# VectorE's order inside gate pairs changed, and sparse attention's angles made one down part earlier

## The reference, cut to what matters

```
def swiglu(h, w1, w3, w2):
    return (jax.nn.silu(h @ w1) * (h @ w3)) @ w2

def rope_tables(positions, rot_dim):
    inv_freq = ROPE_THETA ** (-jnp.arange(0, rot_dim, 2, dtype=jnp.float32) / rot_dim)
    ang = positions.astype(jnp.float32)[..., None] * inv_freq
    return jnp.cos(ang), jnp.sin(ang)
...
    h = modulate(x, norm_g[l, 0], mod[:, 0, 0], mod[:, 0, 1])
    x = x + 0.5 * mod[:, 0, 2][:, None, :] * swiglu(h, ffn1_w1[l], ffn1_w3[l], ffn1_w2[l])
    h = modulate(x, norm_g[l, 1], mod[:, 1, 0], mod[:, 1, 1])
    y = hybrid_mixer(h, ..., rope_a, rope_i, top_k)
    x = x + mod[:, 1, 2][:, None, :] * y
    h = modulate(x, norm_g[l, 2], mod[:, 2, 0], mod[:, 2, 1])
    x = x + 0.5 * mod[:, 2, 2][:, None, :] * swiglu(h, ffn2_w1[l], ffn2_w3[l], ffn2_w2[l])
```

## Time and profile before

| | us |
|---|---|
| median of 3 runs | 1863.03 (1861.79 to 1863.89) |
| the profiled execution | 1862.07 |
| its span | 1860.30 |
| PE busy | 1837.5 (99%) |
| DVE busy | 1334.8 (72%) |
| ACT busy | 857.3 (46%) |
| POOL busy | 270.8 (15%) |

### The profile page before, as it was taken

How to read it: one execution, slowest core, us unless ns; L and a number is a source line. 1 busy time by engine, 2 the same in 40 slices (tenths; PEclk the granted TensorE clock), 3 DMA queues, 4 the chain that set the end, 5 groups by cost and what they waited for, 6 DMA issues and landing times.

```text
span 1860.3 us, 27681 instructions
## 1 busy us (share of the span) xinstructions
PE 1837.5 (99%) x10112; PEld 1530.2 (82%) x10112; DVE 1334.8 (72%) x2105; ACT 857.3 (46%) x1545; POOL 270.8 (15%) x248
## 2 busy tenths in 40 slices
PE   9999999999999999999999989999999999999999
PEld 7777778888888888798988968757767889899897
DVE  7778456757766666896985886866785788689394
ACT  6465445433232233452643554446655455355262
POOL 0001000001111000151532310100000103154140
PEclk9999999999999999999999999999999999999999
DMA  5211113346666563423332122211111422322213
GB/s 187 91 57 68 60 67 115 136 135 235 227 224 224 183 213 106 159 79 110 114 107 84 49 91 91 82 64 50 47 57 69 159 95 78 135 91 103 85 52 102
DMA packets 58325, 208.25 MB, mean 112 GB/s; under 512 B 6688, under 2 KB 6816, under 8 KB 58208
## 3 DMA queue, kind: packets, MB, share of 16 engines
q1 hardware_dynamic: 47232, 167.67, 26.0%
q0 software_dynamic: 10976, 39.00, 6.4%
HBM read 204.48 MB, written 2.10 MB: 111 GB/s over the span
## 4 chain that ended last, share of the span: by engine, by line
PE 79%; DVE 14%; issue 5%; ACT 1%; DMA 0%; SPq 0%; DVEq 0%; ACTq 0%
PE PS L726 16%; PE PS L728 15%; PE PS L727 15%; DVE LO L2962 5%; PE PS L1451 4%; PE PS L1452 4%; PE PS L1453 4%; PE PS L1223 2%; PE PS L1438 2%; PE PS L1440 2%; PE PS L1439 2%; PE PS L1263 2%; PE PS L1250 1%; DVE LO L2153 1%; DVE HL L3009 1%
## 5 line engine op out<-in xcount | busy, mean ns | idle before, releaser
L1542 ACT ACTIVATE HI<-RAW 128x1024 fp32r<-128x1024 f32 x237 | 250.5, 1058 | 326.9 <-PE PS L728 206.6
L2153 DVE TENSOR_TENSOR LO<-RAW,HI 128x1024 fp32r<-128x1024 f32 x237 | 290.7, 1227 | 131.1 <-ACT HI L1542 129.7
L726 PE MATMUL PS<-XH,HI 128*128 128x512 f32 x848 | 337.9, 398 | 0.0
L728 PE MATMUL PS<-XH,LO 128*128 128x512 f32 x848 | 330.8, 390 | 0.0
L727 PE MATMUL PS<-XL,HI 128*128 128x512 f32 x848 | 330.4, 390 | 0.0
L726 PEld LDWEIGHTS PS<-XH,HI 128*128 128x128 f32 x848 | 159.2, 188 | 39.2 <-issue 7.8
L728 PEld LDWEIGHTS PS<-XH,LO 128*128 128x128 f32 x848 | 159.2, 188 | 34.4
L727 PEld LDWEIGHTS PS<-XL,HI 128*128 128x128 f32 x848 | 159.4, 188 | 31.0
L1438 PE MATMUL PS<-TH,HI 128*128 128x256 f32 x576 | 163.8, 284 | 5.0 <-DVE Y L3037 5.0
L1439 PE MATMUL PS<-TL,HI 128*128 128x256 f32 x576 | 163.0, 283 | 0.0
L1440 PE MATMUL PS<-TH,LO 128*128 128x256 f32 x576 | 162.9, 283 | 0.0
(11 more groups left out here) (478 smaller groups left out, 3853.3 us busy)
## 6 DMA issues: line engine op xcount, KB each, us to landing
RAW<-weights SPq DMA_DIRECT2D x237, 512.0 KB, 3.5
ADA<-ada POOLq DMA_DIRECT2D x72, 512.0 KB, 4.5
SRAW<-weights SPq DMA_DIRECT2D x72, 512.0 KB, 4.3
y_out<-X SPq DMA_DIRECT2D x8, 256.0 KB, 2.0
X<-x_in SPq DMA_DIRECT2D x3, 512.0 KB, 7.6
RAW<-weights SPq DMA_DIRECT2D x4, 256.0 KB, 5.5
X<-x_in SPq DMA_DIRECT2D x2, 256.0 KB, 4.5
COND<-condition POOLq DMA_DIRECT2D x1, 512.0 KB, 4.6
```

What stands on the lines that cost most here:

```text
L726: mm(bank, a, moving[0][:, t, :], start=start, stop=False)
L728: ins = mm(bank, z, moving[0][:, t, :], start=False, stop=stop)
L1542: A(HI[n0 % 3][:], RAW[n0 % 3][:], ACT.Copy).then_inc(sem("hi_ready"), 1)
L2153: V.tensor_tensor(LO[n0 % 3][:], RAW[n0 % 3][:], HI[n0 % 3][:].bitcast(F32), ALU.subtract)\
```

## The change

Four things move, and no matmul, transfer or POOL instruction does.

1. Angles. They are made in the second down part of f = 1 (down products 1 and 4) and kept in `T[:, 1, :]` and `UP_ZERO`. The conversion of the positions stands in its down product 0. The tables stay in the third down part, from products 0 and 2 to 1 and 3, behind the copies for the norm.
2. Finishing products. The three multiplies L3024, L3032, L3041 become two: the whole `H[0]` (128x512) behind c12, and the late half of `H[1]` behind A22's own multiply (`last_quarter`, two products behind).
3. Low parts. They go from three products behind to six: the low part of `H[0]` (`low_of_first`) now comes in the next gate pair, the low part of `H[1]` (`low_of_second`) in front of the next odd c11. At the end of a part all that is left comes behind the last A22.
4. ACT. The early silu of a gate pair and the high part of `H[1]` come four products behind in place of two.

The waits that keep buffers apart change with it: A11 of an odd pair waits for `h21_made`, c11 and c22 of odd pairs for low parts of the tiles before, c22 of even pairs for the last multiply.

```diff
+        ANGLE = [Y[:, 0, :], Y[:, 0, :], T[:, 1, :], UP_ZERO[:]]
...
                     elif kind == "A11" and p > 1:
-                        pe.wait_ge(sem("hid"), hid_count(f, pair_tile(p - 2, 1)))
+                        pe.wait_ge(sem("h21_made"), NPAIRS // 2 * (f - 1) + p // 2)
...
                         if s > 2 * v0 + 1:
                             later(f, s - 2)
+                        if s > 2 * v0 + 3:
+                            silu_of_first(f, s - 4)
+                            high_of_second(f, s - 4)
...
-                            if m in (0, 2):
+                            if m in (1, 3):
+                                act.wait_ge(sem("hid_lo"), FT * f + FT)
                                 table(2 + m // 2, (TAB_A2, TAB_I2)[m // 2])
...
                 if kind == "A12":
                     v.wait_ge(*product_done(f, kind, p))
                     v.wait_ge(sem("p1_copied"), of_pair(f, p))
+                    if p % 2:
+                        v.wait_ge(sem("hid_lo"), split_count(f, pair_tile(p - 2, 0)))
                     V.tensor_tensor(dst[0][:, EARLY], P1C, bank, ALU.add).then_inc(sem("c11_made"), 1)
-                    if p % 2:
-                        v.wait_ge(sem("c11_made"), of_pair(f, p))
-                        v.wait_ge(sem("part_silu"), part_silu(f, p, 1))
-                        V.tensor_tensor(H[0][:, EARLY], H[0][:, EARLY], G[0][:, EARLY], ALU.mult)
...
-                        V.tensor_tensor(H[0][:, LATE], H[0][:, LATE], G[0][:, LATE], ALU.mult)\
-                            .then_inc(sem("hid"), 1)
+                        V.tensor_tensor(H[0], H[0], G[0], ALU.mult).then_inc(sem("hid"), 1)
...
+                    if p % 2 == 0 and p:
+                        v.wait_ge(sem("hid"), hid_count(f, pair_tile(p - 1, 1)))
+                    elif p:
+                        v.wait_ge(sem("hid_lo"), split_count(f, pair_tile(p - 2, 1)))
                     V.tensor_tensor(dst[1][:, LATE], P5C, bank, ALU.add).then_inc(sem("c22_made"), 1)
-                    if p % 2:
-                        v.wait_ge(sem("c22_made"), of_pair(f, p))
-                        v.wait_ge(sem("part_silu"), part_silu(f, p, 3))
-                        V.tensor_tensor(H[1][:, LATE], H[1][:, LATE], G[1][:, LATE], ALU.mult)
...
+            def last_quarter(f, s):
+
+                kind, p = PRODUCTS[s]
+                if kind == "A22" and p % 2:
+                    v.wait_ge(sem("c22_made"), of_pair(f, p))
+                    V.tensor_tensor(H[1][:, LATE], H[1][:, LATE], G[1][:, LATE], ALU.mult).then_inc(sem("hid"), 1)
...
-                        if s > 2 * v0 + 2:
-                            later(f, s - 3)
+                        if s > 2 * v0 + 1:
+                            last_quarter(f, s - 2)
+                        if s > 2 * v0 + 5:
+                            low_of_first(f, s - 6)
+                            low_of_second(f, s - 6)
...
                     after_product(f, 2 * v1 - 1)
-                    for s in range(2 * v1 - 3, 2 * v1):
-                        later(f, s)
+                    last_quarter(f, 2 * v1 - 1)
+                    for s in range(2 * v1 - 6, 2 * v1):
+                        low_of_first(f, s)
+                        low_of_second(f, s)
...
-                        if squares and m == 0:
+                        if part == 1 and f == 1 and m == 0:
                             v.wait_ge(sem("pos_loaded"), 32)
                             link(V.tensor_copy(POS2[:], POS2[:].bitcast(I32)))
-                            angles(2, POS2[:], "freq_a")
-                        if squares and m == 2:
-                            angles(3, POS2[:], "freq_i")
+                        if part == 1 and f == 1 and m in (1, 4):
+                            angles(2 + m // 4, POS2[:], ("freq_a", "freq_i")[m // 4])
```

More of the change, by code:

```diff
@@ L1683, in later @@
                 kind, p = PRODUCTS[s]
-                if p % 2 == 0 and kind == "A12":
-                    act.wait_ge(sem("c11_made"), of_pair(f, p))
-                    A(G[0][:, EARLY], G[0][:, EARLY], ACT.Silu).then_inc(sem("part_silu"), 1)
-                elif p % 2 == 0 and kind == "S4":
+                if p % 2 == 0 and kind == "S4":
                     act.wait_ge(sem("c12_made"), of_pair(f, p))
@@ L1692, in later, with silu_of_first, high_of_second @@
                     A(G[1][:, LATE], G[1][:, LATE], ACT.Silu).then_inc(sem("part_silu"), 1)
-                elif p % 2 and kind in ("S4", "A22"):
-                    m = int(kind == "A22")
-                    hidden_hi(f, pair_tile(p, m), H[m])
+                elif p % 2 and kind == "S4":
+                    hidden_hi(f, pair_tile(p, 0), H[0])
+            def silu_of_first(f, s):
+                kind, p = PRODUCTS[s]
+                if p % 2 == 0 and kind == "A12":
+                    act.wait_ge(sem("c11_made"), of_pair(f, p))
+                    A(G[0][:, EARLY], G[0][:, EARLY], ACT.Silu).then_inc(sem("part_silu"), 1)
+            def high_of_second(f, s):
+                kind, p = PRODUCTS[s]
+                if p % 2 and kind == "A22":
+                    hidden_hi(f, pair_tile(p, 1), H[1])
             def whole_silu(f, t, bank, dst):
@@ L1730, in ffn_by_pairs @@
                     later(f, 2 * v1 - 2)
-                    later(f, 2 * v1 - 1)
+                    for s in range(2 * v1 - 4, 2 * v1):
+                        silu_of_first(f, s)
+                        high_of_second(f, s)
                     for m in range(DT):
@@ L1759, in table @@
             def table(k, tab):
+                angle = ANGLE[k]
                 act.wait_ge(sem("angle"), k + 1)
-                A(tab[:, 1, :], Y[:, 0, :], ACT.Sin)
-                A(Y[:, 1, :], Y[:, 0, :], ACT.Abs).then_inc(sem("absolute"), 1)
+                A(tab[:, 1, :], angle, ACT.Sin)
+                A(Y[:, 1, :], angle, ACT.Abs).then_inc(sem("absolute"), 1)
                 act.wait_ge(sem("absolute"), k + 1)
@@ L2312, in angles @@
             def angles(k, pos, freq):
-                if k % 2:
+                if k == 1:
                     v.wait_ge(sem("table"), k)
@@ L2321, in angles @@
                                                 op0=ALU.mult, op1=ALU.add))
-                V.tensor_scalar(Y[:, 0, :], Y[:, 1, :], 3.1415925, -3.1415925, ALU.min, ALU.max)\
+                V.tensor_scalar(ANGLE[k], Y[:, 1, :], 3.1415925, -3.1415925, ALU.min, ALU.max)\
                     .then_inc(sem("angle"), 1)
@@ L3044, in after_product, with low_of_first, low_of_second @@
                     v.wait_ge(sem("part_silu"), part_silu(f, p, 4))
-                    V.tensor_tensor(H[1][:, EARLY], G[1][:, EARLY], bank, ALU.mult).then_inc(sem("hid"), 1)
-            def later(f, s):
+                    V.tensor_tensor(H[1][:, EARLY], G[1][:, EARLY], bank, ALU.mult).then_inc(sem("h21_made"), 1)
+            def last_quarter(f, s):
                 kind, p = PRODUCTS[s]
-                if p % 2 and kind in ("S4", "A22"):
-                    m = int(kind == "A22")
-                    hidden_lo(f, pair_tile(p, m), H[m])
+                if kind == "A22" and p % 2:
+                    v.wait_ge(sem("c22_made"), of_pair(f, p))
+                    V.tensor_tensor(H[1][:, LATE], H[1][:, LATE], G[1][:, LATE], ALU.mult).then_inc(sem("hid"), 1)
+            def low_of_first(f, s):
+                kind, p = PRODUCTS[s]
+                if p % 2 and kind == "S4":
+                    hidden_lo(f, pair_tile(p, 0), H[0])
+            def low_of_second(f, s):
+                kind, p = PRODUCTS[s]
+                if p % 2 and kind == "A22":
+                    hidden_lo(f, pair_tile(p, 1), H[1])
             def whole_hidden(f, t, bank, gate):
@@ L3066, in hidden_zero @@
                     v.wait_ge(sem("unrooted_copied"), 4 * f - 2)
-                    V.tensor_tensor(UP_ZERO[:], UP_ZERO[:], PS[:, 6, :], ALU.mult).then_inc(sem("up_scaled"), 1)
+                    link(V.tensor_tensor(UP_ZERO[:], UP_ZERO[:], PS[:, 6, :], ALU.mult))
                 elif m == 3:
                     v.wait_ge(sem("silu"), FT + 4 * f)
-                    v.wait_ge(sem("up_scaled"), f)
                     V.scalar_tensor_tensor(out=T[:, 0, :], in0=UP_ZERO[:], scalar=SHIFT_COL[1], in1=T[:, 0, :],
```

## The result

| | before | after |
|---|---|---|
| median of 5 runs (us) | 1863.24 (1861.79 to 1863.95) | 1854.81 (1851.76 to 1856.11) |
| span of the profiled execution | 1860.3 | 1853.9 |

The ratio is 0.9949, with an interval of 0.9936 to 0.9963, and the medians lie 8.4 us apart. The forecast was 1855.4, with a range of 1851.0 to 1861.5.

What follows compares the result with a forecast made beforehand. PE bounds the kernel, busy 1837.5 of 1860.3 us. Angles 5.6, S1's copy 3.6, A22 1.8, down starts -3.4 give 7.6 us gained: 1854.5, and 1855.4 with the median 0.96 above the profiled execution; range 1851 to 1861.5.

Steps and rivals of the forecast that it cites:

- Angles: Third down part, first layer: two waits (2.8 and 1.2 us) and a half-clock stretch (1.6) go, 5.6 us gained.
- ScalarE's order: Gate pairs: moving silu and high part behind S2's copy ends 8 waits of S4 for S1's copy, 3.6 us gained.
- The pairs together: Up and gate pairs: two terms, 3.6 us from S1's copy waits and 1.8 from A22's waits for c22.
- The walk of VectorE: VectorE's instructions between c22s in the new order: 11.01 us even to odd, 9.53 odd to even, double pair 20.54.
- What L3024 gives: Up pairs: removing this VectorE multiply gives about 0.6 us of its 1.34, bounds nothing to 1.38.
- Rival 1: Pairs: L3024 gives its whole 1.38 us and A22 waits nowhere; 13.2 us gained, 1849.8 us; chance 14%.
- Rival 2: Pairs give nothing, L3024 wholly under POOL, or lower clock follows idle time at down starts; 1862.0 us; chance 15%.
- Rival 3: VectorE's double pair grows to 21.62 us through the new low part and POOL; slower, 1866.6 us; chance 9%.
- The down starts: Start of the first two down parts, both layers: longer chain behind A22 costs 1.45 us in place of 0.6, 3.4 lost.
- The norm: Norm behind the third down part: its half-clock stretch may fall elsewhere, 1 us left either way.

Runs made afterwards that it cites:

- E1: Kernel before with only the angles moved to the second down part, as in the change; 1857.24 us, ratio 0.9965.
- E9: Kernel before with only ScalarE's early silu of the gate pairs put four products behind in place of two; 1862.43 us, ratio 1.0001.
- E5: Kernel after with the early silu of the gate pairs back two products behind, high part of the second tile left four behind; 1854.0 us, ratio 0.9955.
- E10: Kernel after with the three multiplies and ScalarE's order of before, keeping the new places of angles and low parts; 1858.46 us, ratio 0.9968.
- E7: Kernel before with POOL's four sums of each pair replaced by writes of zeros, so only its times are read; 1850.49 us, ratio 0.993.
- E6: Kernel after with the wide multiply of the first tile split into two narrow ones, behind c11 and c12; 1856.18 us, ratio 0.9964.
- E3: Kernel after with the last pair's first-tile low part right behind its c22 at the end of the first two parts; 1846.94 us, ratio 0.9918.

## Why the prediction was right, and where it was not

The total was right, 1855.4 against 1854.81. By stretches the gain is 9.6 us against the 7.6 of the sum, so that the median came within 0.6 us is partly luck: the terms were off by up to 1.5 us, and the start and the norm, which no term describes, scatter by more than 0.6. Most of the mechanism was as forecast, one attribution was wrong, and several sizes were off.

**Angles, -5.6.** Measured -5.86 (E1 alone -5.86), with nothing lost in the second down part. All three pieces went: the 2.8 of waiting, the stretch at 0.50, and the 1.03.

**ScalarE's order, -3.6.** This step failed, and the total doesn't show it, since VectorE's new order took the same waits away. The waits went, as forecast, but not by this cause: E9 made the same move alone and got 1.0001, with the waits moved to A22 of the gate pair. E5 undid it and lost nothing, and in E10 the waits went without it. The forecast's own paragraph on VectorE said that VectorE sets the pace and that PE's waits are its backlog. It should have asked of every wait in the pairs, not only of A22's, whether it is backlog. What the 8 waits are worth here is what VectorE's double pair gets shorter by (21.30 to 20.6), and the silu's place didn't change that.

**The pairs together, -3.6 and -1.8.** Measured -6.9, 1.5 more than the two terms. The walk of VectorE was right where the backlog stands: 11.01 and 9.53 forecast, 11.02 and 9.59 measured between pairs 9 and 11. What was mis-sized is which pairs reach it. Against E7, where no product waits, a layer of before loses 5.5 us (forecast 5.6) and one of after 2.0 (forecast 2.9): 1.4 of it in pairs 0 to 3, as forecast (1.4), but 0.6 in pairs 4 to 11 (forecast 1.1) and none in 12 to 17 (forecast 0.4). I let VectorE start the second up pair of a part with the full 11.01, but c22 of pair 7 came 10.42 behind that of pair 6.

**What L3024 gives, 0.6.** E6 measures 0.34, its 1.34 us in the profile notwithstanding. It lies within the bounds of 0 and 1.38, nearer to the lower. The rule of the Trainium skill (SBUF — State Buffer, Who interferes with whom), that a VectorE instruction with two SBUF inputs and a GpSimd one that reads SBUF exclude each other, was the better guide here, and E7 agrees with it: with POOL only writing, 0.42 in every pair. Rival 1, which took the 1.34 for work, is refuted by the same runs. Rival 2, by which nothing of L3024 comes back, was about as far off on this size as the forecast (0.34 measured, against 0 and 0.6), but the other moves of the pairs, by subtraction above all the last multiply's, gave what rival 2 denied them, and PE's new idle time at the down starts, 1.45 us, was not followed by a lower clock. Rival 3 needed a longer double pair than 21.30; it was 20.6.

**The down starts, +3.4.** Measured +4.06, 1.02 in each place against 0.85. From A22's first matmul to the down product it is 3.11 us, 1.67 more than its 12 x 0.12, where I had 1.45. The chain of L3059, L3066 and one low part is as forecast; the 0.19 from the end of A22's last 0.12 us (962.48) to L3059 (962.67) was left out. E3 shows that the term was no part of the price of the change: the instruction's earlier place was free.

**The norm.** 0.8 us of the gain lies there, inside the 1 us that the forecast left for it: the half clock stretch is not in the kernel after, yet it is in E1, whose third down part is as short, and in eight more of the 13 traces behind the same 1.7 us of idle time. No edit accounts for it.

## What to carry to other kernels

Where one engine's queue sets the pace, a wait of the engine that it feeds marks a place and not a cause: take away what it names, and the same time comes back at a later product (E9). So price a change by how much it shortens the pacing engine's time over one turn of the loop, here a double pair. The profile's length of an instruction is no measure of what its removal gives when another engine holds it; look for the next instruction that will be held. And when instructions are queued later to relieve a loop, look at the loop's end by itself: there the same instruction is on the path, and an exception to the new order for the last pass gave 6.4 us more (E3).

## What the runs showed of the hardware

- A VectorE multiply with both inputs in SBUF, 128x256, took 0.42 us alone and 1.34 (L3024) to 1.52 (L3066 at 945.81) beside a GpSimd sum of SBUF tiles. The c11 add with an input in PSUM took its 0.41 beside one (L3039 at 931.91 in the kernel after, wholly beside L656; in the earlier trace rows only its last 0.2 us lay beside L655). POOL is held as well: its sums take 1.29 us free and up to 1.68. A GpSimd write without reading (0.52 us) held nothing (E7).
- Behind 2.64 us of idle TensorE in the third down part the granted clock was 0.50 for some 3.4 us, behind 1.03 and behind 1.45 it stayed 1.00. But the length of one idle stretch doesn't tell whether half clock follows: near 748 us PE idles 1.2 us (for RB) in every trace, and a stretch at 0.50 begins within 4 us in 11 of the 13 and not in those of before and E9; behind the 1.7 us in the norm it does in nine of 13. Such a stretch costs 0.5 to 1.2 us in these places, and it comes and goes among executions of one kernel too: of the five of the kernel after, the fastest (1851.76 us) has a mean granted clock of 1.000, the slowest (1856.11) of 0.997, and the others (1854.44 to 1855.59) of 0.998.
- An idle TensorE costs 0.1 to 0.2 us more than the profile's idle time: a wait of 0.22 came with matmuls 0.49 apart where 0.12 is the rule, 0.37 in all (E9, A22 of pair 8).
